# Order of VectorE's work in an attention loop: side work ahead of the next unit's maxima, or behind them

## The reference

```python
c = jnp.cumsum(jax.nn.log_sigmoid(f_logit), axis=1)
for i in range(S // Q_BLOCK):                      # 8 blocks of 128 queries
    q0, q1 = i * Q_BLOCK, (i + 1) * Q_BLOCK
    s = einsum(q[q0:q1], k[:q1]) * dh ** -0.5
    s = s + c[q0:q1] - c[:q1]                      # per head
    s = where(causal mask, s, -1e30)
    p = softmax(s)
    out = einsum(p, v[:q1])
```

## Time and profile before

| | us |
|---|---|
| median of 3 runs | 1435.47 (1435.26 to 1435.56) |
| profiled execution | 1435.38 |
| its span, first to last instruction | 1433.4 |
| TensorE busy | 1410.4 |
| VectorE busy | 1007.4 |
| attention loop, units 0 to 31 | 334 to 510 of the span |

### The profile page before, as it was taken

How to read it: one execution, slowest core, us unless ns; L and a number is a source line. 1 busy time by engine, 2 the same in 40 slices (tenths; PEclk the granted TensorE clock), 3 DMA queues, 4 the chain that set the end, 5 groups by cost and what they waited for, 6 DMA issues and landing times.

```text
span 1433.4 us, 19474 instructions
## 1 busy us (share of the span) xinstructions
PE 1410.4 (98%) x7026; PEld 1162.9 (81%) x7026; DVE 1007.4 (70%) x1460; ACT 644.3 (45%) x1216; POOL 558.4 (39%) x573
## 2 busy tenths in 40 slices
PE   8999999999899999999999999999999999999998
PEld 5878888887688888888888788888888888888886
DVE  7846495646877637877657887767777677795867
ACT  6545343535877653546443532233322322444445
POOL 5743243334545412013012654444444443354402
PEclk9999999999999999999999999999999999999999
DMA  8265264446332298314203113333322335883334
GB/s 212 54 128 119 53 137 99 74 85 210 111 118 90 75 283 193 112 57 127 63 6 136 60 61 105 110 111 110 110 100 93 109 111 198 305 283 99 91 103 147
DMA packets 108105, 173.71 MB, mean 121 GB/s; under 512 B 7485, under 2 KB 63313, under 8 KB 106474
## 3 DMA queue, kind: packets, MB, share of 16 engines
q1 hardware_dynamic: 98976, 148.17, 35.3%
q0 software_dynamic: 5408, 15.76, 4.3%
q10 hardware_dynamic: 3626, 8.54, 1.6%
HBM read 125.42 MB, written 42.30 MB: 117 GB/s over the span
## 4 chain that ended last, share of the span: by engine, by line
PE 87%; POOL 3%; DVE 3%; ACT 3%; DMA 2%; issue 1%; SPq 1%; DVEq 0%; ACTq 0%; POOLq 0%
PE ps L2354 27%; PE ps L2356 27%; PE ps L2355 27%; PE ps L2554 2%; PE ps L2563 1%; DMA w_raw<-in_w_xkv 1%; POOL w_lo L875 1%; PE ps L2592 1%; ACT prob L1340 1%; PE ps L2593 1%; DMA e_raw<-in_w_in 1%; SPq L667 1%; PE ps L2416 1%; DVE prob L1934 1%; PE ps L2729 0%
## 5 line engine op out<-in xcount | busy, mean ns | idle before, releaser
L2354 PE MATMUL ps<-t_lo,s_hi 128*128 128x512 f32 x308 | 119.9, 389 | 0.1
L2356 PE MATMUL ps<-t_hi,s_lo 128*128 128x512 f32 x308 | 119.8, 389 | 0.0
L2355 PE MATMUL ps<-t_hi,s_hi 128*128 128x512 f32 x308 | 119.8, 389 | 0.0
L2354 PE MATMUL ps<-h_lo_T,w_hi 128*128 128x512 f32 x256 | 100.5, 392 | 1.3 <-ACT u_t L1251 1.0
L1549 ACT ACTIVATE s_hi<-w_raw 128x512 fp32r<-128x512 f32 x77 | 48.7, 632 | 118.0 <-PE ps L2356 91.9
L1634 DVE TENSOR_TENSOR s_lo<-w_raw,s_hi 128x512 fp32r<-128x512 f32 x77 | 62.0, 805 | 56.3 <-ACT s_hi L1549 56.3
L2356 PE MATMUL ps<-h_hi_T,w_lo 128*128 128x512 f32 x256 | 99.7, 390 | 0.0
L2355 PE MATMUL ps<-h_hi_T,w_hi 128*128 128x512 f32 x256 | 99.6, 389 | 0.0
L1565 ACT ACTIVATE p_sb<-ps 128x512 f32<-128x512 f32 x22 | 13.0, 598 | 186.6 <-PE ps L2356 186.6
L2354 PE MATMUL ps<-hf_lo_T,w_hi 128*128 128x512 f32 x212 | 82.5, 389 | 0.0
L2355 PE MATMUL ps<-hf_hi_T,w_hi 128*128 128x512 f32 x212 | 82.5, 389 | 0.0
(11 more groups left out here) (403 smaller groups left out, 4373.9 us busy)
## 6 DMA issues: line engine op xcount, KB each, us to landing
w_raw<-hs_dram SPq DMA_DIRECT2D x77, 256.0 KB, 2.8
raw_p<-in_w_ffn_in SPq DMA_DIRECT2D x22, 512.0 KB, 4.6
w_raw<-in_w_ffn_in SPq DMA_DIRECT2D x22, 512.0 KB, 4.3
hs_dram<-h_sum SPq DMA_DIRECT2D x11, 1024.0 KB, 9.0
hs_dram<-hq SPq DMA_DIRECT2D x11, 768.0 KB, 7.1
wq_B<-in_w_ffn_out SPq DMA_DIRECT2D x8, 1024.0 KB, 7.6
raw_f<-in_w_in SPq DMA_DIRECT2D x14, 512.0 KB, 7.3
gate_dram<-c_st SPq DMA_DIRECT2D x28, 256.0 KB, 2.0
```

What stands on the lines that cost most here:

```text
L2354: nc.tensor.matmul(dst, w_h, x_l, start=start, stop=False, skip_group_check=onto)
L2355: nc.tensor.matmul(dst, w_h, x_h, start=False, stop=False, skip_group_check=onto)
L2356: return nc.tensor.matmul(dst, w_l, x_h, start=False, stop=stop, skip_group_check=onto)
```

## The change

VectorE's work of one unit that isn't part of that unit's own softmax (`last_pair`, the mixer's subtraction, `pool_gated` except where it directly follows the maxima, `qk_lo_of` of blocks under 4) becomes a function, `side_work(u)`. It was called at the end of unit u, ahead of unit u + 1's biased scores and maxima. It is now called in unit u + 1, behind the maxima of both heads and ahead of that unit's normalisation. The loop already had one turn more than there are units, so the last unit's side work stands in turn 32. The split of finished outputs (`o_lo_of` in units 25 to 27) stays at the end of the unit. No other engine's list changes.

```diff
--- before.py
+++ after.py
@@ -1920,31 +1920,9 @@
                 dve.wait_ge(o_hi_ready, p + 1)
                 minus_hi(o_lo[p][:], o_sb[:, p, :], o_hi[p][:], o_lo_ready)
 
-            for u in range(PAIRS * T + 1):
+            def side_work(u):
+
                 p, i = divmod(u, T)
-                b, n = u % 2, (i + 1) * P
-                for a in range(2 if u < PAIRS * T else 0):
-                    h = 2 * p + a
-                    dve.wait_ge(sc_done, 2 * u + a + 1)
-                    dve.wait_ge(negc_masked, 2 * (2 * u + a + 1))
-                    if i:
-                        dve.wait_ge(negc_plain, 14 * p + 2 * i + a - 1)
-                    if u >= 2:
-                        dve.wait_ge(pt_done, groups_before(u - 1))
-                    nc.vector.tensor_tensor_reduce(out=prob[b][:, a, 0:n], in0=two(2 * a)[:, 0:n], in1=negc[h % 3][:, 0:n],
-                                                   scale=-1.0, scalar=HIGHEST, op0=ALU.add, op1=ALU.min,
-                                                   accum_out=neg_max[:, b, a:a + 1]).then_inc(sc_biased, 1)
-                if 2 * u in GATED_IN and (i >= 4 or i == 0):
-                    pool_gated(GATED_IN[2 * u])
-                if i >= 4 and u < 3 * T and i - 1 in SPLIT_HI:
-                    e, a0, a1 = SPLIT_HI[i - 1]
-                    qk_lo_of(p + 1, e, (qk_st if p else qk_first)[:, e % 2, :], a0, a1)
-                for a in range(2 if u < PAIRS * T else 0):
-                    dve.wait_ge(exp_ready, 2 * u + a + 1)
-                    nc.vector.reciprocal(prob_inv[:, b, a:a + 1], prob_sum[:, b, a:a + 1]).then_inc(inv_ready, 1)
-                    dve.wait_ge(inv_ready, 2 * u + a + 1)
-                    nc.vector.tensor_scalar(prob[b][:, a, 0:n], prob[b][:, a, 0:n], prob_inv[:, b, a:a + 1], None,
-                                            ALU.mult).then_inc(prob_ready, 1)
                 if u in DEFER_DONE:
                     last_pair(DEFER_DONE[u])
                 for m in MIXED_IN.get(u, ()):
@@ -1960,6 +1938,34 @@
                 if i < 4 and u < 3 * T and i - 1 in SPLIT_HI:
                     e, a0, a1 = SPLIT_HI[i - 1]
                     qk_lo_of(p + 1, e, (qk_st if p else qk_first)[:, e % 2, :], a0, a1)
+
+            for u in range(PAIRS * T + 1):
+                p, i = divmod(u, T)
+                b, n = u % 2, (i + 1) * P
+                for a in range(2 if u < PAIRS * T else 0):
+                    h = 2 * p + a
+                    dve.wait_ge(sc_done, 2 * u + a + 1)
+                    dve.wait_ge(negc_masked, 2 * (2 * u + a + 1))
+                    if i:
+                        dve.wait_ge(negc_plain, 14 * p + 2 * i + a - 1)
+                    if u >= 2:
+                        dve.wait_ge(pt_done, groups_before(u - 1))
+                    nc.vector.tensor_tensor_reduce(out=prob[b][:, a, 0:n], in0=two(2 * a)[:, 0:n], in1=negc[h % 3][:, 0:n],
+                                                   scale=-1.0, scalar=HIGHEST, op0=ALU.add, op1=ALU.min,
+                                                   accum_out=neg_max[:, b, a:a + 1]).then_inc(sc_biased, 1)
+                if u:
+                    side_work(u - 1)
+                if 2 * u in GATED_IN and (i >= 4 or i == 0):
+                    pool_gated(GATED_IN[2 * u])
+                if i >= 4 and u < 3 * T and i - 1 in SPLIT_HI:
+                    e, a0, a1 = SPLIT_HI[i - 1]
+                    qk_lo_of(p + 1, e, (qk_st if p else qk_first)[:, e % 2, :], a0, a1)
+                for a in range(2 if u < PAIRS * T else 0):
+                    dve.wait_ge(exp_ready, 2 * u + a + 1)
+                    nc.vector.reciprocal(prob_inv[:, b, a:a + 1], prob_sum[:, b, a:a + 1]).then_inc(inv_ready, 1)
+                    dve.wait_ge(inv_ready, 2 * u + a + 1)
+                    nc.vector.tensor_scalar(prob[b][:, a, 0:n], prob[b][:, a, 0:n], prob_inv[:, b, a:a + 1], None,
+                                            ALU.mult).then_inc(prob_ready, 1)
                 if u in (25, 26, 27):
                     o_lo_of(u - 25)
 
```

## The result

The change makes the kernel slower: 1456.53 us (median of 4 runs, 1456.44 to 1458.35) against 1435.51 (4 runs, 1435.26 to 1436.71), ratio 1.0147 with a 95% interval of 1.0135 to 1.0159. The forecast was 1453 us, range 1446 to 1458.

What follows compares the result with a forecast made beforehand. The prediction took TensorE, busy 98% of the span, as the bound, so its waits are paid in full. It added 6.4 us (units 0 to 15) and 11.3 us (units 16 to 31), 17.7 in all, to 1435.4: 1453 us, range 1446 to 1458.

Steps and rivals of the forecast that it cites:

- What bounds the kernel: Whole kernel: TensorE is busy 98% of the span, so everything that makes it wait is paid in full.
- No change: Rival: later idle time takes up the attention loop's shift; 1435 to 1437 us, chance 0.03.
- Half the price: Rival: TensorE's idle time absorbs the shift of units 0 to 15, only later waits stand; 1445 us, chance 0.12.
- One wait: Unit 31: two maxima, the sum and 0.15 take 3.2 us from VectorE being free; TensorE waits 2.3 us.
- The first half, 6.4 us: Units 0 to 15: 3.0 up to unit 13, 1.7 in unit 14, 1.8 in unit 15, 0.1 back.
- The walk: Unit-by-unit timing of units 1 to 15: TensorE's shift +1.4 at unit 1, +2.2 at unit 2, +3.0 at unit 13.
- Units 16 to 31, 11.3 us: Attention loop's second half: TensorE's waits for deferred sums in units 19, 20, 21, 23, 25, 27, 29, 31 total 11.3 us.
- the reason given: Unit 20: its maxima start late behind GpSimd, so only 0.1 us was counted.
- The sum: Whole attention loop: 6.4 + 11.3 = 17.7 us, nothing given back behind it, 1453 us.
- The clock: Attention loop: TensorE's granted clock stays 1.00 through pauses up to 1.4 us; no cost was counted for it.
- Clock: Rival: 1.2 GHz for about 1 us of work after each of ten pauses, some 10 us more; 1463 us, chance 0.03.
- Faster: Rival: attention loop's maxima and exponentials start earlier; TensorE regains at most 3.0 us, 1432.4 us, chance 0.04.

Runs made afterwards that it cites:

- The kernel with one pass in front instead of two: Against the changed kernel, the side work stands between the maxima of the first head and those of the second: 1444.04 us, ratio 1.0057.
- the kernel with all waits filled: The changed kernel plus unused TensorE matmuls ahead of each step that waited 1.38 us or more (units 1, 5, 14, 15, 21, 23, 27, 29, 31): 1453.79 us.
- four gates deferred: Against the kernel before, only the gated products in the side work of units 17, 19, 25 and 27 moved behind the next unit's maxima: 1437.64 us, ratio 1.0013.
- filling the two waits: The changed kernel plus ten unused TensorE matmuls in each of units 14 and 23, ahead of the product step that waits for the bank: 1453.52 us.
- the last pair's kernel: Against the kernel before, only the last pair's four sums moved behind the next unit's two maxima: 1440.62 us, ratio 1.0033; profiled again, 1438.99 us.

## Why the prediction was right, and where it was off

- **What bounds the kernel.** Right. Behind the loop the same stretch holds the same work, and the shift at the loop's end (20.60 us and unit 0's 0.72) is the loss. That puts *No change* out. *Half the price* (1445) is out too: the first half's shift of 8.4 us stood to the end.
- **One wait.** Right: 3.12 us from VectorE being free to TensorE's start, forecast 3.2. The kernel with one pass in front instead of two shows that it is the passes that are paid.
- **The first half, 6.4 us.** Without falls of the clock (the kernel with all waits filled) it was 7.0: 3.6 up to unit 14 instead of 3.0 (3.3 in the changed kernel), then 2.1 for unit 14 instead of 1.7, 1.4 for unit 15 instead of 1.8, and 0.1 back. The walk hit its points: TensorE's step in unit 1 at 341.77 (forecast 341.65), in unit 2 at 346.95 (346.85), in unit 5 at 360.54 (360.55), each less the 0.72. It was mis-sized at the maxima of unit 14, which came at 408.04 on that count, not at 407.16: VectorE was 3.2 us late there, not 2.3. The prediction let VectorE's lag stand from unit 2 on; in both kernels the maxima of unit 14 wait for GpSimd, which has just done a split of a weight that waited for ScalarE. That split came 3.2 us later (403.17 - 0.72 against 399.27); why ScalarE was late wasn't followed further. GpSimd's timeline before:

```profile
399.27 2.40 POOL L875 TENSOR_TENSOR w_lo<-w_raw,w_hi 128x1024 fp32r<-128x1024 f32 x1 [2.09 <-ACT w_hi L1144]
```

and GpSimd's and VectorE's in the changed kernel:

```profile
403.17 2.42 POOL L875 TENSOR_TENSOR w_lo<-w_raw,w_hi 128x1024 fp32r<-128x1024 f32 x1 [4.01 <-ACT w_hi L1144]
...
408.76 1.09 DVE L1953 CUSTOM_DVE_ANT_0 prob<-ps,negc 128x896 f32<-128x896 f32 x1 [0.79 <-POOL negc L981]
```

- **Units 16 to 31, 11.3 us.** Without falls of the clock 10.7. Unit 19 took 1.2 (1.2), unit 21 1.5 (1.6), unit 25 1.0 (0.9), unit 27 1.8 (1.7), unit 29 1.5 (1.6), unit 31 2.2 (2.3), unit 23 1.5 instead of 1.9. Unit 20 took nothing (0.1), but not for the reason given: in the changed kernel its maxima don't start late behind GpSimd, and where they do, with four gates deferred, the unit costs 1.2.
- **The sum.** Without falls of the clock the order costs 17.7 us, forecast 17.7. That is luck in part: the errors of the terms, up to 0.6 us, had both signs.
- **The clock.** This is the step that failed, though the time stayed in the range. The prediction argued that the clock had stayed at 1.00 through pauses up to 1.4 us, and took nothing for pauses up to 2.3; *Clock*, with a chance of 0.03, had ten falls of about 1 us each. What came were two falls of some 1.6 us, and they make the difference between the 20.6 of the changed kernel and the 17.7 of the one without falls; filling the two waits took 3.0 us off the time. The reasoning went beyond its rows: a pause of 1.4 us said nothing about one of 2.0. The Trainium skill ("TensorE: Matmul & The Clock Gate", section "Why this matters for your kernels") warns of pauses between bursts of matmuls, but only of longer ones than any here. By it no fall was to be expected; the trace disagrees, with falls behind two of the nine pauses of 1.38 to 2.00 us.
- **Faster.** Out, but its mechanism was there in small: the waits for maxima and scores fell by 2.3 us, and where only the q/k subtractions are deferred TensorE is 0.75 us earlier in the trace, too little to show in the runs. VectorE's idle time ahead of reciprocals, forecast to fall well under 26 us, was 28.0: it doesn't measure what the order costs or gives.

## What to carry to other kernels

An engine with 30% idle time still has work that is urgent: what empties a bank is urgent if its user comes right behind the instruction that the emptying now waits for. Compare two spans for each such bank, from the last free moment of the emptying engine to its end, and from there to its user's arrival, and price each deferral by the passes that are put ahead of it, not by its own length. A pause of TensorE can cost more than its length: in these traces the clock fell behind a quarter of the pauses of 1.38 to 2.0 us, and behind none of those of 0.80 to 1.29 us. A filler of useless work in front of a wait can then be faster than idling: here it gave 3.0 us.

## What the runs showed of the hardware

- In the attention loops of the 14 traces of this case there are 44 pauses of TensorE of 1.38 to 2.0 us with a releaser. Behind 11 of them the granted clock fell to 0.50 (1.2 GHz) for three to four microseconds, beginning 0.2 to 1.4 us after work had resumed. Behind none of 34 pauses of 0.80 to 1.29 us did it. Within 1.38 to 2.0 us length does not pick them: one of 1.41 us was followed by a fall, while of the pauses of about 2.0 us that of unit 23 was in all three traces that have it, and that of unit 31 in none of four. Nor does the program alone: the last pair's kernel fell at two places in one trace and at one in the other. What picks them stays open. The Trainium skill ("TensorE: Matmul & The Clock Gate", section "Part 1: The HAM clock gate") says that one kernel can show different numbers of slow matmuls at its start from run to run. The last pair's kernel shows such a difference in its middle, two falls in one trace and one in the other; the changed kernel's two traces, with the same two falls, don't.
- What a fall costs depends on what comes next. Behind units 14 and 23 it was some 1.6 us, behind unit 1 too (a final shift of 5.1 us against 3.5 in the two traces of the last pair's kernel). Behind unit 5, after which TensorE waits for VectorE again anyway, 0.55 us were left of it at unit 8 (a shift of 3.59 us in the kernel with units 14 and 23 filled, which fell there, and 3.04 in the changed kernel, which didn't).
